# Recurrence outputs gated inside the recurrence's later steps, first mixer tiles split beside the last projection units, new state stored last

## The reference

```
h   = rms_norm(x, g) * (1 + scale1) + shift1
z   = h @ w_in            # u_f, u_p, q, k, v, o, gate inputs, merge
y_f = fourier_mix(u_f) @ w_proj_f
y_p = pool_mix(u_p)    @ w_proj_p
hf, Cf, nf, mf = mlstm_dir(q, k, v, ...)             # scan forwards, chunk by chunk
hb, Cb, nb, mb = mlstm_dir(rev(q), rev(k), rev(v), ...)   # scan backwards
y_m = (sigmoid(o) * (hf + rev(hb))) @ w_proj_m
y   = (sig(gF) * y_f + sig(gP) * y_p + sig(gM) * y_m) @ w_out
x   = x + gate1 * rms_norm(y)
x   = x + gate2 * rms_norm(swiglu(...))
```

## Time and profile before

| | us |
|---|---|
| median of 3 runs (lowest, highest) | 1938.36 (1938.07, 1941.24) |
| the profiled execution, its own time | 1944.64 |
| its span, first to last instruction | 1943.1 |
| PE busy | 1840.8 (95%) |
| DVE, ACT, POOL busy | 852.1, 713.7, 224.0 |

### The profile page before, as it was taken

One profiled execution on the slowest core, in us unless ns is written; L12 is line 12 of the kernel. 1 busy time (PEld: TensorE's weight loads), 2 busy tenths in 40 slices (PEclk: granted clock), 3 DMA queues, 4 the chain that ended last, 5 costly groups with the idle time before them and its releaser, 6 DMA issues.

```text
span 1943.1 us, 28168 instructions
## 1 busy us (share of the span) xinstructions
PE 1840.8 (95%) x10615; PEld 1778.5 (92%) x10615; DVE 852.1 (44%) x1290; ACT 713.7 (37%) x1085; POOL 224.0 (12%) x305
## 2 busy tenths in 40 slices
PE   6799999999999999689898999999999999999995
PEld 4599999989999999679788999999999999999994
DVE  6410102333344344266978564444554444643333
ACT  2321213232222222145564545444445444433331
POOL 0400001312122222332412000000000000000000
PEclk9899999999999999789999999999999999999997
DMA  5555446654455544877563443344443444444430
GB/s 213 211 207 171 141 146 214 222 167 139 133 167 167 166 166 139 221 281 243 160 201 119 140 130 121 128 135 136 130 152 122 127 141 134 127 151 129 130 120 33
DMA packets 94406, 305.06 MB, mean 157 GB/s; under 512 B 11119, under 2 KB 25378, under 8 KB 94192
## 3 DMA queue, kind: packets, MB, share of 16 engines
q1 hardware_dynamic: 52816, 191.80, 30.3%
q0 software_dynamic: 19664, 64.89, 10.8%
q10 hardware_dynamic: 21840, 47.19, 6.9%
HBM read 253.72 MB, written 50.11 MB: 156 GB/s over the span
## 4 chain that ended last, share of the span: by engine, by line
PE 84%; DVE 6%; DMA 5%; ACT 2%; issue 1%; POOL 1%; SPq 0%; ACTq 0%; DVEq 0%; POOLq 0%
PE bank L484 26%; PE bank L486 25%; PE bank L485 25%; DMA raw<-in_w_stream 1%; DVE y L1545 1%; PE bank L628 1%; DMA hf_sb<-h_scratch 1%; DVE w_lo L1466 1%; DMA o_sb<-z_scratch 1%; PE bank L865 1%; PE bank L868 1%; PE bank L657 1%; PE bank L875 1%; PE bank L883 1%; DVE yy_lo L1814 1%
## 5 line engine op out<-in xcount | busy, mean ns | idle before, releaser
L484 PE MATMUL bank<-h_hi,w_hi 128*128 128x384 f32 x2136 | 737.1, 345 | 9.9 <-DVE h_lo L1932 7.3
L485 PE MATMUL bank<-h_lo,w_hi 128*128 128x384 f32 x2136 | 724.9, 339 | 0.0
L486 PE MATMUL bank<-h_hi,w_lo 128*128 128x384 f32 x2136 | 724.5, 339 | 0.0
L1466 DVE TENSOR_TENSOR w_lo<-raw,w_hi 128x1024 fp32r<-128x1024 f32 x306 | 380.5, 1245 | 538.8 <-ACT w_hi L1082 536.2
L1082 ACT CAST w_hi<-raw 128x1024 fp32r<-128x1024 f32 x306 | 320.3, 1048 | 521.0 <-PE bank L486 386.2
L484 PEld LDWEIGHTS bank<-h_hi,w_hi 128*128 128x128 f32 x2136 | 405.5, 190 | 26.8 <-ACT z_st L1158 10.1
L485 PEld LDWEIGHTS bank<-h_lo,w_hi 128*128 128x128 f32 x2136 | 405.3, 190 | 0.8
L486 PEld LDWEIGHTS bank<-h_hi,w_lo 128*128 128x128 f32 x2136 | 404.7, 189 | 0.0
L1158 ACT ACTIVATE z_st<-bank 128x384 f32<-128x384 f32 x132 | 64.3, 490 | 341.4 <-PE bank L486 341.3
L486 PE MATMUL bank<-f_hi,w_lo 128*128 128x384 f32 x528 | 177.4, 336 | 0.0
L484 PE MATMUL bank<-f_hi,w_hi 128*128 128x384 f32 x528 | 177.4, 336 | 0.0
(11 more groups left out here) (241 smaller groups left out, 1787.7 us busy)
## 6 DMA issues: line engine op xcount, KB each, us to landing
raw<-in_w_stream SPq DMA_DIRECT2D x297, 512.0 KB, 3.6
z_scratch<-z_st ACTq DMA_DIRECT2D x44, 576.0 KB, 3.1
raw<-in_w_ada SPq DMA_DIRECT2D x48, 512.0 KB, 5.7
mg<-z_scratch ACTq DMA_DIRECT2D x24, 576.0 KB, 5.3
zt<-z_scratch POOLq DMA_DIRECT2D x27, 256.0 KB, 3.7
x_scratch<-xT POOLq DMA_DIRECT2D x8, 576.0 KB, 13.4
raw<-in_k_dft SPq DMA_DIRECT2D x9, 512.0 KB, 3.5
kv_scratch<-kv_st POOLq DMA_DIRECT2D x9, 512.0 KB, 4.7
```

Source lines behind the costliest of these rows:

```text
L484: pe.matmul(out, a_hi, b_hi, start=start, stop=False)
L485: pe.matmul(out, a_hi, b_lo, start=False, stop=False)
L486: return pe.matmul(out, a_lo, b_hi, start=False, stop=stop)
L1466: dve.tensor_tensor(w_lo[:, slot], raw[:, slot], w_hi[:, slot].bitcast(F32), ALU.subtract).then_inc(s_wlo, 1)
```

## The change

Tiles are now taken in the order in which the two directions finish them. From chunk index 5 on, each step of the recurrence ends with the four transposes of one tile on PE, the gating of that tile and the sum of the next one on DVE; POOL's loads of the sums and of the o gate, and its stores of gated tiles, go between the chunk loads of the steps. Seven tiles are turned inside the steps, tiles 7 and 8 after parts 0 and 1 of `hm`. The context tile's two results are added straight from `num` and are no longer stored in `h_scratch`. The o gate's sigmoid is applied when its four projection units leave PSUM. The mixer tiles of group 0 are split beside parts 1 to 5. `mx_in` has two slots for three, projection parts use three banks for four. The new state is stored after the last mixer load of group 0. `xT2` is loaded in `E2` of group 0 instead of `E1`. Loops over steps are written out. Tiles lie elsewhere in SBUF so that these things can overlap.

```diff
-HM_TILES = ((), (0, 1), (2, 3), (4, 5), (6, 7), (8,))
+HM_TILES = (3, 4, 2, 5, 1, 6, 0, 7, 8)
+HM_FIRST = 5
+HM_AFTER = (7, 8)
-MG, MX = 3, 3
+MG, MX = 3, 2
+        MX_PARTS = ((), (0, 1), (2, 3), (4, 5), (6,), (7,))
...
+        def hm_turned(x):
+            n = x - (2 * HM_FIRST + 1)
+            return n if n >= 0 else None
+        def hm_summed(x):
+            n = x - 2 * HM_FIRST
+            return n if n >= 0 else None
...
-                    pe.wait_ge(s_zev, zi * 3 + b - 3)
+                    pe.wait_ge(s_zev, zi * 3 + b - 2)
-                    m = mm3(pe, bank[j % 4][:, 0:GW], ...)
+                    m = mm3(pe, bank[b][:, 0:GW], ...)
...
                 ml_state(i, d)
+                n = hm_turned(2 * i + d)
+                if n is not None:
+                    h_turn(n)
+
+            def h_turn(n):
+                pe.wait_ge(s_hs, n + 1)
+                if n:
+                    pe.wait_ge(s_ho, n)
+                for h in range(H):
+                    m = pe.transpose(bank[3][:, ktile(h)], hf_sb[:, n % 2, 0, ktile(h)], ident)
+                m.then_inc(s_ht, 1)
...
-                            m = mm3(pe, bank[3 * (c0 % 2) + b][:, 0:GW], ...)
+                            m = mm3(pe, bank[3 - 3 * (c0 % 2) + b][:, 0:GW], ...)
...
-                    z_evac(zi, zi, SHIFT_A, part % NG)
+                    z_evac(zi, zi, SHIFT_A, part % NG, func=ACT.Sigmoid)
...
+                    if part:
+                        for k in MX_PARTS[part]:
+                            mx_piece(0, k)
...
                 if g == 0 and c_from == 0:
-                    for u in range(3):
-                        act.wait_ge(s_host[u], 16 * NT // 3)
-                    act.wait_ge(s_new, 80)
                     for u in range(2):
                         act.wait_ge(s_zst[u], 8 * (Z_COUNT - 1))
+                    act.wait_ge(s_host[0], 16 * 5)
+                    act.wait_ge(s_host[1], 16 * 4)
...
-                    if g == 0:
-                        act.dma_start(xT2[:, c], x_dram[c]).then_inc(s_back, 16)
...
+                    if g == 0:                       # in e2
+                        if c == 0:
+                            act.wait_ge(s_new, 80)
+                        act.dma_start(xT2[:, c], x_dram[c]).then_inc(s_back, 16)
...
                 m.then_inc(s_cup, 1)                 # end of DVE's ml_step
+                turned, summed = hm_turned(x), hm_summed(x)
+                if turned is not None:
+                    h_gate(turned)
+                if summed is not None:
+                    h_sum(summed)
...
+            def hm_load(n):                          # POOL
+                c = HM_TILES[n]
+                t = slice(c * P, (c + 1) * P)
+                if c < NT - 1:
+                    if n >= 2:
+                        pool.wait_ge(s_ht, n - 1)
+                    pool.dma_start(hf_sb[:, n % 2], both[c]).then_inc(s_hl[n % 2], 16)
+                if n >= 2:
+                    pool.wait_ge(s_host[n % 2], 16 * (n // 2))
+                pool.dma_start(o_sb[:, n % 2], z_dram[16:20, :, t].rearrange("a p t -> p a t")).then_inc(s_ol[n % 2], 16)
...
+            for i in range(1, NT):
+                for d in range(2):
+                    ml_store(i - 1, d)
+                    ml_load(i, d, False)
+                if i >= HM_FIRST:
+                    n = 2 * (i - HM_FIRST)
+                    for d in range(2):
+                        pool.wait_ge(s_hst[d], 16 * i)
+                    for m in range(n, n + 2):
+                        if m >= 2:
+                            hm_store(m - 2)
+                        hm_load(m)
+            hm_store(NT - 3)
+            hm_load(NT - 1)
+            pool.wait_ge(s_kvm, 2 * NT)
             for k in range(MX):
                 mx_load(k)
...
+            hm_store(NT - 2)
+            hm_store(NT - 1)
+            pool.wait_ge(s_host[0], 16 * 4)
             for k in range(MX, KT):
                 mx_load(k)
+            for d in range(2):
+                pool.wait_ge(s_cup, 2 * NT - 1 + d)
+                pool.dma_start(new_C[0, 0, d]..., st_ctx[:, d, :, 0:DH]).then_inc(s_new, 16)
+                pool.dma_start(new_n[0, 0, d]..., st_ctx[:, d, :, DH], allow_slow_non_contiguous=True).then_inc(s_new, 16)
+            pool.dma_start(new_m[0], mnew[0:1, :, NT - 1]).then_inc(s_new, 16)
```

More of the change, by code:

```diff
@@ L194, in build @@
         s1 = ExitStack()
-        cst = sb(s1, "cst", [P, CB_W])
-        K = {n: cst[:, s] for n, s in CB.items()}
+        cst = sb(s1, "cst", [P, CB["pool"].start])
+        s1h = ExitStack()
+        hf_sb = sb(s1h, "hf_sb", [P, 2, 2, MW])
+        s1h.close()
+        cst_p = sb(s1, "cst_p", [P, CB_W - CB["pool"].start])
+        K = {n: cst[:, s] for n, s in CB.items() if n not in ("pool", "cb")}
+        for n in ("pool", "cb"):
+            K[n] = cst_p[:, CB[n].start - CB["pool"].start:CB[n].stop - CB["pool"].start]
         s1r = ExitStack()
@@ L258, in build @@
         s2m = ExitStack()
+        num = sb(s2m, "num", [P, 2, H, C1])
         q_sb = sb(s2m, "q_sb", [P, 2, H, P])
@@ L691, in z_part @@
                         unit_ready(z_number(zi, shift))
-                j = 3 * zi0 + b
-                if not (first and j < 4):
-                    pe.wait_ge(s_zev, zi * 3 + b - 3)
+                if not (first and zi0 == 0):
+                    pe.wait_ge(s_zev, zi * 3 + b - 2)
                 for k in range(KT):
@@ L914, in hm @@
                     z_part(ZI_H + part // NG, ZI_H + part // NG, SHIFT_B, part % NG)
[L915 to L924, removed]
+                    if part < len(HM_AFTER):
+                        h_turn(HM_AFTER[part])
             def mixers():
@@ L1255, in mixers @@
                         act.wait_ge(s_ga, 6)
[L1257 to L1264, removed]
+                for i in range(NT - 1):
+                    for d in range(2):
+                        ml_step(i, d, ZI_M + 2 * i + d, ZI_M + 2 * i + d)
                 for d in range(2):
@@ L1758, in ml_step, with h_sum, h_gate @@
                 m.then_inc(s_cup, 1)
-            def mlstm():
[L1761 to L1765, removed]
+                turned, summed = hm_turned(x), hm_summed(x)
[3 more added lines that the diff above has]
+                    h_sum(summed)
+            def h_sum(n):
+                out = hf_sb[:, n % 2, 0]
+                if n == NT - 1:
+                    dve.wait_ge(s_ht, n - 1)
+                    dve.wait_ge(s_hd, 2 * NT)
+                    dve.tensor_tensor(out.rearrange("p (h e) -> p h e", h=H), num[:, 0, :, 0:DH], num[:, 1, :, 0:DH],
+                                      ALU.add).then_inc(s_hs, 1)
+                else:
+                    dve.wait_ge(s_hl[n % 2], 16 * (n // 2 + 1))
+                    dve.tensor_tensor(out, out, hf_sb[:, n % 2, 1], ALU.add).then_inc(s_hs, 1)
+            def h_gate(n):
+                dve.wait_ge(s_ht, n + 1)
+                dve.wait_ge(s_ol[n % 2], 16 * (n // 2 + 1))
+                o = o_sb[:, n % 2].rearrange("p h t -> p (h t)")
+                dve.tensor_tensor(o, o, bank[3][:, :], ALU.mult).then_inc(s_ho, 1)
+            def mlstm():
                 dve.wait_ge(s_ga, 6)
                 dve.wait_ge(s_st0, 64)
-                turn(0, True)
-                with dve.Fori(1, (NT - 1) // 2) as t:
-                    turn(t, False)
+                for i in range(NT - 1):
+                    for d in range(2):
+                        n = ZI_M + SHIFT_B + AHEAD + 2 * i + d
+                        ml_step(i, d, st_lat, i == 0, n, n)
                 for d in range(2):
@@ L1779, in mlstm @@
                         split(n, n)
[L1780 to L1790, removed]
-                        dve.tensor_tensor(ho[:, c % 3].rearrange("p h t -> p (h t)"),
-                                          o_sb[:, c % 3].rearrange("p h t -> p (h t)"), bank[5 + c % 3][:, :],
-                                          ALU.mult).then_inc(s_ho, 1)
+                    if part < len(HM_AFTER):
+                        h_gate(HM_AFTER[part])
+                    for k in MX_PARTS[part]:
+                        mx_piece(0, k)
             def mx_piece(g, k):
```

142 lines of the change are left out of this document (48 added, 94 removed), and 2 rows, old and new, of the table ORDER.

## The result

The changed kernel takes **1918.72 us** (median of four runs, 1912.32 to 1920.02) against 1938.39 before: ratio 0.989, 95% interval 0.9869 to 0.991. In a later series it was 0.9882 (0.9863 to 0.9902; 1917.56 against 1940.85). The forecast was 1916, with a range of 1902 to 1927. The profiled execution took 1919.05 us, span 1917.2, where the one before took 1944.64 and 1943.1.

What follows compares the result with a forecast made beforehand. PE's waits bound the kernel, then the chain of transfers; only 780.69 to 855.86 us could be won. Unit 2's 25.0 us, less 1.5 clock and 1.0 residual, gave 22.5: 1938.4 to 1915.9 us, range 1902 to 1927.

Steps and rivals of the forecast that it cites:

- (a): Forecast case: old waits go, PE waits once, for unit 0's gated results behind the new state's stores; 1916, chance 0.50.
- (b): Rival: the slow stretch does not touch ACT's store and gates; 33 us saved, 1905, chance 0.26.
- PE: Steps to `E1` unit 2: a turned tile adds 0.44 us; PE ready at 818.9 against 855.86, 37.0 us.
- DVE, ACT, POOL: In the steps: sums, gatings and later chunk loads stay hidden; 0 us, bound 2 us for each of two steps.
- (d): Rival, slower: POOL's round becomes the step, six later steps 7.3 us longer each; net 21 us slower, 1960, chance 0.04.
- (e): Rival: turned tiles make the steps wait as long as `hm` did, and the time stays; 1938, chance 0.05.
- Mixer tiles: Group 0's pairs, 5 us each, hidden beside the parts; last low half ready near 811.5; costs 0 to 2 us.
- The new state: `new_n` stores slow the last `z_scratch` store and first `mg` load, 8.4 us each; unit 2 starts at 830.9.
- two slow stretches in a row: After `new_n` issues at about 807.7 and 809.3, transfers slow from about 810 to 829, taken at 70 GB/s.
- The clock: PE idle for 12 us before unit 2 makes its clock fall; 1.5 us charged (0 to 2.2).
- The residual: `xT2` loads, moved out of group 0's `E1` and queued ahead, delay group 1's first `mg` load; 1.0 us (0 to 2.7).
- The sum: Whole kernel: 25.0 less 1.5 for the clock, less 1.0 for the residual, 22.5 us saved; median 1915.9.

Runs made afterwards that it cites:

- n_later: Changed kernel with only the two `new_n` stores moved behind the adds of group 0's first `E1` unit; 1916.26 us, ratio to before 0.9871.
- n_out: Changed kernel without the two `new_n` stores, that output left unwritten; 1913.97 us, ratio to before 0.9856.
- n_turned: Changed kernel with `new_n` turned by PE, copied by ACT and stored as 8 pieces of 512 bytes; 1914.35 us, ratio to before 0.987.
- mx_behind: Changed kernel with group 0's eight mixer tiles split behind the last projection part, not beside the parts; 1934.11 us, ratio to before 0.997.
- x_in_e1: n_turned with the residual loaded in `E1` of group 0 again, from its second unit on; 1912.12 us, ratio to before 0.9858.

## Why the prediction was right

**The case was the forecast one** (a): the old waits go, and PE waits once, for unit 0's gates behind a `z_scratch` store slowed by `new_n`. n_later, n_out and n_turned show that cause; in (b) the wait would have been the 3 us that they have.

**PE.** A turned tile costs 0.45 us of a step, where I took 0.44. `E1` was put at 810.6 and began at 808.68; ready for unit 2 at 818.9, measured 817.16 without a wait: 38.7 us ahead of before instead of 37.0. But 1.5 of this is not the change's: in this execution the recurrence began 0.6 us earlier, and its first step was 0.9 us shorter (17.99 against 18.89).

**DVE, ACT, POOL.** No step waits for a tile; from the second step's scores to `hm` are 275.53 us after and 272.44 before, 3.1 more, as charged. (d) and (e) are out.

**Mixer tiles.** Hidden, as said: the last low half was ready at 810.88 (811.5 predicted). mx_behind shows that the edit I had costed at nothing matters: 17.1 us without its cover, the slow gates included.

**The new state.** Issued 3.4 us earlier than I said: `hm` began 1.5 us earlier than in my sum, and a pair takes 4.0 to 4.5 us and not 5. The store took 9.34 us (8.4 predicted), at 65 GB/s (70). But I had two slow stretches in a row, until 829. Here the two stores of `new_n` landed 7.7 and 9.6 us after their issue, at 812.1 and 815.5: the stretches lay over each other, and all was over at about 819, so the gates loaded in 4.30 us and not 8.4, and unit 2 started at 826.02, not 830.9. This is the term that was mis-sized: 29.8 us saved at that point instead of 25.0. Of the 4.9 between them the gates are 4.1 and the earlier issue of the `z_scratch` store 1.9; the store itself takes 0.9 back. In a row does occur: in mx_behind the two stores landed at 829.2 and 836.3, and the transfers were slow twice (columns as in the earlier trace rows):
```profile
820.00:831.00 11.00, 7.56 (x31) 7.04 (x30) 2.34 (x3) 3.35 (x4) 2.83 (x5) 0.72 0.83 92
831.00:835.00 4.00, 0.00 (x0) 0.00 (x0) 0.00 (x0) 0.54 (x1) 0.00 (x0) 0.74 1.08 224
835.00:841.00 6.00, 3.64 (x11) 3.67 (x12) 3.28 (x4) 1.56 (x2) 2.79 (x2) 0.50 0.92 111
```
What decides between the two isn't shown.

**The clock.** 2.3 us (7% of 32.98) for 1.5, just over its bound of 2.2.

**The residual.** The size was near, 1.85 us (units 0 to 2 of group 1 lie 11.06 us apart, 9.21 before) for 1.0, but the mechanism was wrong. I had the gates' load land late because it is queued behind `xT2`: it lands in 5.70 us, 5.53 before. It is issued late: 2.46 us after unit 0 began, against 0.77 before, because ACT first splits the last mixer tile, which the residual's traffic delayed. ACT's timeline after, and x_in_e1, show it:
```profile
888.92 0.51 ACT L1315 CAST mx_hi<-mx_in 128x384 fp32r<-128x384 f32 x1 [1.63 <-DMA mx_in<-mix_scratch]
889.07 0.38 ACTq L1332 DMA_DIRECT2D mg<-z_scratch  x1
```

**The sum.** 29.8 less 2.3 less 1.9 is 25.6, what the two profiled executions differ by; I had 22.5. Of the 25.6, 1.5 lie in front of the recurrence's second step and 24.1 are the stretch. (In the sum for (b), 814.4 + 6.75 is 821.15 and not 821.3; nothing hangs on it.) That the median still came out above mine is the other side: before's profiled execution was 6.3 us above its median, that of after 0.3, so between the medians lie 19.7 us, 23.3 in the later series. Such an execution of before is not rare: in the later series they spread from 1933.60 to 1945.46 us. So the mechanism was right, but that the median came within 3 us of the forecast is partly luck.

## What to carry to other kernels

Look at the piece, not the bytes: a small store that is read 4 bytes at a time belongs where no transfer is urgent, or is made dense first. Moving it beside other urgent transfers only moves the stall. When a tail of work is spread under earlier steps, ask of each queue what now comes last on it; here the next wait stood behind a store that the first gates didn't read. And of a transfer that "has room" in another stage, ask which short-slotted stream shares that stage.

## What the hardware showed that I had not expected

While the two 2 KB stores of 4-byte pieces are under way, the packets of other queues are held up in the middle: of the 128 packets of 4.6 KB of the `z_scratch` store, 30 took over 1 us, the longest 4.3, where in n_turned all took under 0.2. The packets of `new_n` itself, 128 bytes each in all forms but the last, don't explain it: read 4 bytes at a time they took 0.20 us in the changed kernel and 0.04 in n_later, from a dense tile 0.03. In the kernel before, the last packet of the store issued at 766.89 is over at 769, and the transfers stay slow until 779. What holds them up in between, no run shows.
